# Latent queries of a hybrid trunk in six tiles ahead of the gate input, rotary exchange moved to the key side

## The reference

```python
z = h @ o_w_in[i]
c_u, c_v, cq, ckv, kr = jnp.split(z, O_SPLITS, axis=-1)          # 512, 512, 384, 256, 32 columns
yc = spatial_gating(gelu(c_u), gelu(c_v), o_spatial[i], ...)      # u * (W v + bias), v normed
q = (rmsnorm(cq, q_a_gain) @ w_uq).reshape(b, s, 8, 64 + 32)      # 8 heads, 64 plain and 32 rotary
kv = (rmsnorm(ckv, kv_a_gain) @ w_ukv).reshape(b, s, 8, 64 + 64)
q_nope, q_rope = rmsnorm(q[..., :64], ...), rmsnorm(q[..., 64:], ...)
k_nope, k_rope = rmsnorm(kv[..., :64], ...), rmsnorm(kr, ...)     # k_rope is shared by the heads
x -> [x1 * cos - x2 * sin, x2 * cos + x1 * sin]                   # apply_rope, on q_rope and k_rope
o = softmax(chunk-causal q k^T * 96 ** -0.5) @ v
```

## Time and profile before

| | |
|---|---|
| median of 3 runs | 1105.24 us (1104.94 to 1105.44) |
| profiled execution | 1105.54 us |
| its span | 1103.7 us |
| PE busy | 1095.3 us (99%) |
| DVE busy | 550.1 us (50%) |
| ACT busy | 419.0 us (38%) |
| POOL busy | 103.6 us (9%) |
| TensorE clock granted | 1.00 |

### The profile page before, as it was taken

How to read it: one execution, slowest core, us unless ns; L and a number is a source line. 1 busy time by engine, 2 the same in 40 slices (tenths; PEclk the granted TensorE clock), 3 DMA queues, 4 the chain that set the end, 5 groups by cost and what they waited for, 6 DMA issues and landing times. The chain is left out here.

```text
span 1103.7 us, 13745 instructions
## 1 busy us (share of the span) xinstructions
PE 1095.3 (99%) x5148; PEld 881.6 (80%) x5148; DVE 550.1 (50%) x778; ACT 419.0 (38%) x665; POOL 103.6 (9%) x126
## 2 busy tenths in 40 slices
PE   9999999999999999999999999999999999999998
PEld 7777788888888888888878765788888888888887
DVE  6677957344334433242466589655334433453321
ACT  5556436333223222131446558545223322332110
POOL 6000000010001000000102023000001100100000
PEclk9999999999999999999999999999999999999999
DMA  7512233332333333332233200232333233227441
GB/s 227 171 58 85 69 111 99 96 95 92 98 95 95 95 96 98 100 100 88 72 96 92 85 20 2 77 117 93 98 97 102 85 114 95 95 77 173 112 125 47
DMA packets 103241, 106.00 MB, mean 96 GB/s; under 512 B 26267, under 2 KB 79968, under 8 KB 103200
## 3 DMA queue, kind: packets, MB, share of 16 engines
q1 hardware_dynamic: 85488, 103.04, 30.2%
q10 hardware_dynamic: 16656, 2.10, 1.2%
q0 software_dynamic: 1056, 0.30, 0.1%
HBM read 101.23 MB, written 2.10 MB: 94 GB/s over the span
## 5 line engine op out<-in xcount | busy, mean ns | idle before, releaser
L1131 DVE TENSOR_TENSOR w_lo<-raw,w_hi 128x1024 fp32r<-128x1024 f32 (+2 forms) x192 | 224.7, 1176 | 419.7 <-ACT w_hi L702 417.4
L702 ACT ACTIVATE w_hi<-raw 128x1024 fp32r<-128x1024 f32 (+2 forms) x192 | 194.6, 1018 | 467.1 <-PE ps L1690 434.5
L1688 PE MATMUL ps<-h_hi,w_hi 128*128 128x512 f32 x912 | 359.7, 394 | 0.3 <-DVE h_lo L1155 0.3
L1689 PE MATMUL ps<-h_lo,w_hi 128*128 128x512 f32 x912 | 355.1, 389 | 0.0
L1690 PE MATMUL ps<-h_hi,w_lo 128*128 128x512 f32 x912 | 355.1, 389 | 0.0
L1688 PEld LDWEIGHTS ps<-h_hi,w_hi 128*128 128x128 f32 x912 | 171.2, 188 | 41.1 <-issue 5.6
L1689 PEld LDWEIGHTS ps<-h_lo,w_hi 128*128 128x128 f32 x912 | 171.2, 188 | 36.3 <-issue 1.7
L1690 PEld LDWEIGHTS ps<-h_hi,w_lo 128*128 128x128 f32 x912 | 171.2, 188 | 36.1
L585 POOL TENSOR_TENSOR ffn_t<-ffn_t,row_scale 128x512 f32<-128x512 f32 x40 | 50.9, 1294 | 606.4 <-ACT ffn_t L892 606.4
L1689 PE MATMUL ps<-w_lo,act_hi 128*128 128x512 f32 (+1 forms) x178 | 68.8, 387 | 0.0
L1690 PE MATMUL ps<-w_hi,act_lo 128*128 128x512 f32 (+1 forms) x178 | 68.8, 387 | 0.0
(11 more groups left out here) (293 smaller groups left out, 1155.6 us busy)
## 6 DMA issues: line engine op xcount, KB each, us to landing
raw<-in_w_ffn_in SPq DMA_DIRECT2D x88, 512.0 KB, 3.5
raw<-in_w_ffn_out SPq DMA_DIRECT2D x44, 512.0 KB, 3.7
raw<-in_e_w_in SPq DMA_DIRECT2D x17, 512.0 KB, 3.8
raw<-in_o_w_in SPq DMA_DIRECT2D x8, 512.0 KB, 3.7
raw<-in_o_w_out SPq DMA_DIRECT2D x8, 512.0 KB, 3.6
raw<-in_e_w_out SPq DMA_DIRECT2D x8, 256.0 KB, 3.9
raw<-in_e_w_out SPq DMA_DIRECT2D x4, 512.0 KB, 4.5
out_tok<-x_blocks ACTq DMA_DIRECT2D x16, 128.0 KB, 2.5
```

The source lines that it names most:

```text
L702: ins = act.activation(dst, src, ACT.Copy)
L1131: ins = TT(dst, src, high, ALU.subtract)
L1688: MM(dst, st_hi, mv_hi, start=start, stop=False)
L1689: MM(dst, st_hi, mv_lo, start=False, stop=False)
```

## The change

The query weights come as three loads in place of four: load 104 holds the 64 plain columns of heads 0 to 3, load 105 the 32 rotary columns of all eight heads, load 107 the plain columns of heads 4 to 7. That makes six tiles: four with two heads' plain rows (`q_nope`), two with four heads' rotary rows (`q_rope`). ACT squares them and copies them out of PSUM with the gain. All six are computed before the second c_u load; the two sums and two spreads stand inside c_u loads. `q_scale` multiplies the plain rows in 64-row pieces into each head's tile and the rotary tiles in place. The rotary rows are then written twice into a head's tile, 32 rows at a time: times the cosines on POOL, times the sines on DVE (`q_shift`, to the neighbouring 32 rows). The exchange of halves moves to the shared key: `turn_keys` replaces `turn` in the matmul that adds up the rotated key. `q_nope` lies in the memory of `u_c`. The gate products wait for one u_c tile at a time, and the value tiles stand earlier. POOL's weight swaps are gone; the tables come in five DMAs; a selection matrix `sel32` for 32-row groups is made at the start by four small matmuls. The loads behind are numbered one lower.

```diff
-O_UQ, O_CU = (104, 105, 110, 111), (106, 107, 108, 109)
-N_LOADS = 188
...
+O_UQ, O_CU = (104, 105, 107), (106, 108, 109, 110)
+N_LOADS = 187
...
+    def rope_row(h):
+        return 64 * (1 - h % 2) + 32 * (h // 2 % 2)
...
-            he, ho = 96 * 2 * j, 96 * (2 * j + 1)
-            sp.dma_start(dst[:, :, 0:96], src[:, :, he:he + 96]).then_inc(raw_landed[n % 2], 16)
-            sp.dma_start(dst[:, :, 128:160], src[:, :, ho + 64:ho + 96]).then_inc(raw_landed[n % 2], 16)
-            sp.dma_start(dst[:, :, 192:256], src[:, :, ho:ho + 64]).then_inc(raw_landed[n % 2], 16)
+            if j == 1:
+                for h in range(HEADS):
+                    c = P * (h // 4) + rope_row(h)
+                    sp.dma_start(dst[:, :, c:c + 32], src[:, :, 96 * h + 64:96 * h + 96]).then_inc(raw_landed[n % 2], 16)
+            else:
+                for i in range(4):
+                    h = 2 * j + i
+                    sp.dma_start(dst[:, :, 64 * i:64 * i + 64], src[:, :, 96 * h:96 * h + 64]).then_inc(raw_landed[n % 2], 16)
...
+        pool.wait_ge(means_loaded, 16)
+        pool.memset(mean32[:, :], 0.0).then_inc(columns_set, 1)
+        pool.wait_ge(columns_set, 2)
+        for a in range(0, P, 32):
+            pool.memset(mean32[a:a + 32, a:a + 32], 1 / 32).then_inc(columns_set, 1)
...
-        def uq_swap(j):
...
-        uq_swap(0)
-        uq_swap(1)
         pool.wait_ge(kr_rotated, 1)
-        pool.wait_ge(uq_columns, 2)
         for n, h in enumerate((0, 2, 4, 6, 1, 3, 5, 7)):
             a = 64 * (1 - h % 2)
             if n == 4:
                 pool.wait_ge(kr_copied, 4)
             pool.tensor_copy(o_k[a:a + 64, h, :], kr[a:a + 64, 1, :]).then_inc(kr_copied, 1)
         pool.wait_ge(kr_copied, HEADS)
-        uq_swap(2)
-        uq_swap(3)
+        for h in range(HEADS):
+            a = rope_row(h)
+            pool.wait_ge(oq_scaled, 5 + h // 4)
+            pool.tensor_tensor(o_q[a:a + 32, h, :], q_rope[a:a + 32, h // 4, :], tables[a:a + 32, TAB_KEY:TAB_KEY + S], ALU.mult
+                               ).then_inc(oq_turned, 1)
...
+        act.wait_ge(means_loaded, 16)
+        blocks = [t.rearrange("p (r c) -> p r c", r=2) for t in (turn_keys[:, :], turn)]
+        for to, of, sign in ((slice(0, 32), slice(0, 32), 1.0), (slice(32, 48), slice(48, 64), -1.0), (slice(48, 64), slice(32, 48), -1.0)):
+            act.activation(blocks[0][:, :, to], blocks[1][:, :, of], ACT.Copy, scale=sign).then_inc(join_ready, 1)
...
-        def q_squares(j, b0):
+        def q_tiles(j, b0):
 
             act.wait_ge(load_used, O_UQ[j] + 1)
             for i in range(2):
-                h = 2 * j + i
-                if h >= 4:
+                t = 2 * j + i
+                if t >= 4:
                     act.wait_ge(sums_ready, M_OQ + 1)
-                elif h >= 2:
+                elif t >= 2:
                     act.wait_ge(spatial_turned, 2)
-                act.activation(q_sq(h), ps[:, b0 + i, :], ACT.Square).then_inc(oq_squared, 1)
+                act.activation(q_sq(t), ps[:, b0 + i, :], ACT.Square).then_inc(oq_squared, 1)
+            for i in range(2):
+                dst = q_rope[:, i, :] if j == 1 else q_nope[:, j + i, :]
+                act.activation(dst, ps[:, b0 + i, :], ACT.Copy, scale=g_col(G_OQR if j == 1 else G_OQN)).then_inc(oq_gained, 1)
...
+        q_tiles(2, 6)
         through(107)
+        rms(M_OQ + 1, ps[:, 5, :], 1)
+        through(108)
         gelu_table()
         through(109)
         for j in range(4):
             act.wait_ge(u_scaled, j + 1)
             act.activation(u_c[:, j, :], u_c[:, j, :], ACT.Gelu_apprx_tanh).then_inc(u_ready, 1)
-        q_squares(2, 4)
-        through(110)
+        act.wait_ge(u_ready, 1)
         rms_table()
-        q_squares(3, 6)
+        key_squares(0)
         yc_square(0)
         yc_square(1)
-        key_squares(0)
-        rms(M_OQ + 1, ps[:, 3, :], 1)
+        act.wait_ge(oq_turned, HEADS)
+        act.wait_ge(oq_scaled, 18)
+        key_squares(1)
+        key_gains_1()
         yc_square(2)
         yc_square(3)
-        key_squares(1)
-        key_gains_1()
...
-        def q_tiles(j, b0):
-            for i in range(2):
-                h = 2 * j + i
-                dve.wait_ge(oq_squared, h + 1)
-                tab = TAB_ODD if h % 2 else TAB_EVEN
-                STT(out=o_q[:, h, :], in0=ps[:, b0 + i, :], scalar=g_col(G_OQO if h % 2 else G_OQE),
-                    in1=tables[:, tab:tab + S], op0=ALU.mult, op1=ALU.mult).then_inc(oq_turned, 1)
-        def q_scale(r, banks):
+        def q_scale(r):
 
             dve.wait_ge(rs_spread, r + 1)
             dve.sem_inc(rs_used, 1)
-            for g, b in enumerate(banks):
-                h = 4 * r + g
-                TT(o_q[:, h, :], ps[:, b, :], o_q[:, h, :], ALU.mult).then_inc(oq_scaled, 1)
+            dve.wait_ge(oq_gained, 6 if r else 4)
+            for h in range(4 * r, 4 * r + 4):
+                a = 64 * (h % 2)
+                TT(o_q[a:a + 64, h, :], ps[a:a + 64, 4 + h // 2 % 2, :], q_nope[a:a + 64, h // 2, :], ALU.mult
+                   ).then_inc(oq_scaled, 1)
+            if r == 0:
+                for i in range(2):
+                    TT(q_rope[:, i, :], ps[:, 6 + i, :], q_rope[:, i, :], ALU.mult).then_inc(oq_scaled, 1)
+        def q_shift(h):
+            a = rope_row(h)
+            b = a - 32 if h // 2 % 2 else a + 32
+            dve.wait_ge(oq_scaled, 6)
+            TT(o_q[b:b + 32, h, :], q_rope[a:a + 32, h // 4, :], tables[a:a + 32, TAB_TURN:TAB_TURN + S], ALU.mult
+               ).then_inc(oq_scaled, 1)
 
...
-        q_tiles(0, 4)
-        through(104)
-        q_tiles(1, 6)
-        through(106)
+        through(105)
         rms(M_OQ, ps[:, 4, :], 1)
...
+        through(106)
         through(107)
-        q_scale(0, (4, 5, 6, 7))
+        rms(M_OQ + 1, ps[:, 5, :], 1)
         through(108)
+        q_scale(0)
+        for h in range(4):
+            q_shift(h)
+        q_scale(1)
         dve.wait_ge(load_used, O_CU[3] + 1)
+        dve.wait_ge(oq_scaled, 14)
         for j in range(4):
             TT(u_c[:, j, :], ps[:, j, :], row_scale[:, :], ALU.mult).then_inc(u_scaled, 1)
         through(109)
-        q_tiles(2, 4)
-        through(110)
+        for h in range(4, HEADS):
+            q_shift(h)
         dve.wait_ge(gate_bias_loaded, 32)
-        dve.wait_ge(gates_mixed, 1)
         for j in range(4):
+            dve.wait_ge(gates_mixed, j + 1)
             STT(out=yc[:, j, :].rearrange("p (n i) -> p n i", n=QT), in0=ps[:, j, :].rearrange("p (n i) -> p n i", n=QT),
                 scalar=g_col(G_V + j), in1=gate_bias[:, j:j + 1, :].broadcast_to([P, QT, P]),
                 op0=ALU.mult, op1=ALU.add).then_inc(gates_ready, 1)
         yc_gate(0)
         yc_gate(1)
-        q_tiles(3, 6)
+        key_gains_0()
         yc_gate(2)
         yc_gate(3)
-        key_gains_0()
-        rms(M_OQ + 1, ps[:, 3, :], 1)
         yc_sum(1)
         yc_sum(2)
-        q_scale(1, (0, 1, 2, 3))
...
-        def spread(m, banks):
+        def spread(m, banks, ropes=0):
 
             pe.wait_ge(rs_ready, m + 1)
             for g, b in enumerate(banks):
-                ins = MM(ps[:, b, :], sel[32 * g:32 * g + 32, :], rs_of(m)[32 * g:32 * g + 32, :], start=True, stop=True)
+                w = sel32 if g >= len(banks) - ropes else sel
+                ins = MM(ps[:, b, :], w[32 * g:32 * g + 32, :], rs_of(m)[32 * g:32 * g + 32, :], start=True, stop=True)
...
-        def q_sums(r, bank):
-            pe.wait_ge(oq_turned, 4 * r + 4)
-            sums4(bank, [(mean_odd if g % 2 else mean_even)[:, 48:80] for g in range(4)], [q_sq(4 * r + g) for g in range(4)])
+        def q_sums_0():
+            pe.wait_ge(oq_gained, 4)
+            sums4(4, [mean64[:, 48:80]] * 2 + [mean32[:, 0:P:4]] * 2, [q_sq(t) for t in range(4)])
+        def q_sums_1():
+            pe.wait_ge(oq_squared, 6)
+            sums4(5, [mean64[:, 48:80]] * 4, [q_sq(t) for t in (4, 5, 4, 5)])
+        def q_spread_0():
+            pe.wait_ge(rs_step, M_OQ + 2)
+            pe.wait_ge(oq_gained, 6)
+            spread(M_OQ, (4, 5, 6, 7), 2)
+        def q_spread_1():
+            pe.wait_ge(oq_scaled, 4)
+            spread(M_OQ + 1, (4, 5))
 
         def cu_load(j, extra=None):
             load(O_CU[j], plain(512, 4), (2 * j, 2 * j + 1), H, range(4), j == 0, j == 3, extra=extra)
...
         q_load(1, 6)
         pe.wait_ge(cv_ready, 4)
         cu_load(0)
-        q_sums(0, 4)
-        cu_load(1)
-        spread(M_OQ, (4, 5, 6, 7))
-        cu_load(2)
-        cu_load(3)
-        pe.wait_ge(oq_scaled, 2)
-        q_load(2, 4)
-        pe.wait_ge(u_scaled, 4)
+        q_sums_0()
+        q_load(2, 6)
+        cu_load(1, q_sums_1)
+        cu_load(2, q_spread_0)
+        cu_load(3, q_spread_1)
         pe.wait_ge(cv_normed, 4)
         for g0 in range(0, 8, 2):
+            pe.wait_ge(u_scaled, g0 // 2 + 1)
             for t, g in ((t, g) for t in range(QT) for g in (g0, g0 + 1)):
```

(22 more changed lines are left out.)

78 lines of the change are left out of this document (37 added, 41 removed).

## The result

The changed kernel takes **1111.14 us** (median of 5 runs, 1111.01 to 1111.69) against 1105.44 for the kernel before in the same comparison: a ratio of 1.0052, 95% interval 1.0041 to 1.0063. It is slower by 5.7 us. The forecast was 1109.0 with a range of 1104.0 to 1110.3: the side was right, the size was 2.1 us short, and the result lies 0.84 us above the range. All medians here are over runs with a mean granted clock of 0.997 or more; one run of experiment 1, at 0.655, took 1569.52 us and is left out.

The account below looks back on a forecast made before the run. PE, busy 1095.3 of 1103.7 us, was taken as the bound, the stage's cost set by when ACT begins the key root. 1105.54 + 0.25 (start) + 3.5 (later root) = 1109.3, against the median 1109.0; range 1104.0 to 1110.3.

Parts of the forecast that it names:

- What bounds the stage: In the rewritten stage (594 to 658 us), the moment ACT begins the key square root (647.45) decides the cost.
- PE, 4.08 us less: Query loads on PE: four loads of 18 matmuls become three, 18 x 0.2265 = 4.08 us less PE work.
- The general rule: Anywhere but at PE's few waits, a removed matmul is worth its pitch (0.2265 us), unless a wait takes its place.
- Turn-taking: DVE's first four sines alternate with POOL's cosine products, 1.65 us a round: about 6.0 us instead of 2.8.
- the first wait: Before the first of DVE's four sine products beside POOL, DVE waits 0.5 us.
- Rival 2: DVE holds the port over its four sines or is not held at all: no change, 1105.8 us; chance 0.33.
- Rival 3: The end hangs on PE, so the saved matmuls arrive: 1101.4 us; chance of over 0.2% faster 0.1.
- Rival 1: POOL's pieces on four partition quarters run side by side, eight in about 2.9 us: +2.45, 1107.9 us; chance 0.2.
- From u_c to the root, 14.2 us: From DVE's start of u_c to ACT's key root: 10.3 us of DVE steps, then ACT squares and gains, 14.2 in all.
- The start, 0.25: Four more small matmuls on PE at 40 us cost between 0 and 0.42 us, taken as 0.25.
- At nothing: Six more ACT copies, dropped POOL copies, 16 query weight transfers, tables in five transfers and memsets were taken to cost nothing.
- the forecast's own sign of being wrong: The forecast is wrong if, among other signs, any load of query weights is waited for on a DMA.

Follow-up runs that it names:

- experiment 1: Changed kernel, with all eight POOL cosine products waiting until DVE has done its first four sine products: 1110.15 us.
- Run 8: Changed kernel, with the key root ahead of the last two gate squares on ACT and the third-square sum behind the root's two steps on DVE: 1111.27 us.
- run 11: Changed kernel with sines read from PSUM, ACT making the first key gains, root ahead of second gains and two gate squares, low part and POOL gains later: 1105.93 us.
- Run 2: Changed kernel, with POOL's eight cosine products replaced by zero fills of the same pieces that read nothing: 1105.57 us.
- run 6: Changed kernel in its own DVE order, with sines reading rotary tiles scaled in PSUM and two ACT copies to SBUF for POOL: 1106.20 us.
- run 12: On top of run 11: gate squares around the root, second key gains on DVE, low part behind the first two scaled keys: 1105.74 us.
- run 4: Changed kernel, with DVE's first four sine products moved so that all eight stand behind u_c and the low part: 1111.12 us.
- run 5: Changed kernel, with sines read from PSUM, two ACT copies for POOL, and the first four sines behind the second four 64-row pieces: 1110.48 us.
- run 3: Changed kernel plus 20 unread matmuls on PE directly behind the last gate input load, filling its wait for u_c: 1109.63 us.

## Why the prediction was right or wrong

- **What bounds the stage** (the key root on ACT): right as a measure in the changed kernel (root +5.63, spread +5.53, span +5.5 us), too strong as "decides". Run 8 took the root 1.1 us earlier (0.9 with the start taken off) and gained nothing between the medians, and in run 11 the gate mean held the end. Two chains arrive together, the root's and the gate mean's.
- **PE, 4.08 us less**: right, and it was worth nothing, as the forecast's sum had it. Run 2 has no collision at all and equals before. The general rule in the same text, that a matmul removed is worth its pitch unless a wait takes its place, met its exception here.
- **Turn-taking**: right, and this is the step that carried the sign. A mean of 1.60 us for a sine (6.41 for four; forecast 1.65 a round, 6.0 for the four), POOL start to start 1.67. I had taken 0.5 for the first wait, it was 0.67, and every round was a little longer: 0.4 us short. The row that gave the full wait, the scaling at 681.89, has only one tensor operand in SBUF, so it was not a pair of the kind it stood for; the one row of that kind, the low part at 595.14, had lost 0.27. That the price fitted all the same is shown by the runs, not by those rows. Runs 2 and 6 exclude that the 32 rows, the shift of partitions or POOL's writing does it: the operand in SBUF does. Rival 2 falls with that; its time, 1105.8, is that of a kernel without collision in this order (1105.57 and 1106.20).
- **Rival 3** (the saved matmuls arrive): fell. Even without a collision, and with the lists reordered around the root (runs 11 and 12), the end stays where it was.
- **Rival 1** (pieces side by side): fell. Alone (runs 4 and 5), POOL's pieces on different quarters of the partitions start 1.33 to 1.37 us apart and take 1.26 to 1.29 each, as the two in 2.54 of the earlier trace rows.
- **From u_c to the root, 14.2 us**: this step failed. It measured 15.17. The sum took the gate products at the 3.71 us of the earlier trace rows, a row at granted clock 1.00, though the same text let PE stand idle for 4 us ahead of them. They took 5.38, at a granted 0.50. The forecast had PE through with both key halves 9.9 us behind u_c, waiting; it measured 12.0, and ACT waited 0.68 us for PE instead. With PE kept busy (run 3) the distance was 14.14 and the time 1109.63. This term is 1.0 us in the profile, and 1.5 to 1.8 between the medians.
- **The start, 0.25**: the four matmuls added what was said (0.26 more shift between 15 and 40 us), but this profiled run had already begun 0.51 late, from a wait for h_lo. Over the thirteen runs with these matmuls the shift at 40 us is 0.30 in the mean, from -0.51 to 0.82. So the 0.5 us belong more likely to this profiled run than to the change; how much of it the medians hold is not shown.
- **Range**: start 0.5, sines 0.4 and clock 1.0 add up to the 1.9 us between the 3.75 forecast at the root and its 5.63. The range's upper end had 1.3 for slower pieces and nothing for the clock.
- **At nothing**: right for PE, which waits for no load of query weights; the six ACT copies delay nothing either. But the forecast's own sign of being wrong, a load of query weights waited for on a DMA, did show once: at 578.26 ACT had waited 1.88 us for the transfers of one. The sign had been set too wide, since ACT had waited in the same place before (2.22 us, for POOL's swaps in `raw`), and PE lost nothing by either.

## What to carry to other kernels

Before work is moved to GpSimd to relieve VectorE, look for the VectorE operations that will lie beside it with both operands in SBUF; here four of them took 3.6 us more, while the same products with one operand in PSUM took no more than alone. Where a change lets TensorE stand idle for some us, price what follows the gap at half clock too. And a saving on the engine that is busy 99% is worth only what moves the wait that ends last: count the lists of the other engines between two such waits before removing a matmul.
